# Strips of eight weight pieces: high and low passes ordered by pairs of pieces instead of by single pieces

## What is computed

```
block 1: proj   = x @ w_in                          # 2048 -> 12800
         r, i   = sigmoid(per-head u @ w_a), sigmoid(per-head u @ w_x)   # 20 heads, two directions
         h      = scans over time of (a(r), i*u)    # forward and backward
         merged = sig(g_lru) * (h @ w_lru_out) + sig(g_conv) * (conv @ w_conv_out)
         h1     = layer_norm(ALPHA*x + merged @ w_o)
         h2     = layer_norm(ALPHA*h1 + relu(h1 @ mlp_w1 + b1)**2 @ mlp_w2 + b2)
block 2: proj   = rms_norm(h2) @ w_in_2             # three attention / convolution branches
         x2     = h2 + mix @ w_out_2
         out    = x2 + (silu(n @ w_gate) * (n @ w_up)) @ w_down,   n = rms_norm(x2)
```

## Time and profile before

| what | us |
|---|---|
| median of three runs | 2660.29 (2658.74 to 2661.93) |
| the profiled execution, its own time | 2661.17 |
| its span in the trace | 2659.4 |
| busy: PE / DVE / ACT / POOL | 2641.6 / 1750.2 / 1349.3 / 34.5 |
| granted TensorE clock over the span | 0.999 of 2.4 GHz |

### The profile page before, as it was taken

How to read it: one execution, slowest core, us unless ns; L and a number is a source line. 1 busy time by engine, 2 the same in 40 slices (tenths; PEclk the granted TensorE clock), 3 DMA queues, 4 the chain that set the end, 5 groups by cost and what they waited for, 6 DMA issues and landing times.

```text
span 2659.4 us, 40669 instructions
## 1 busy us (share of the span) xinstructions
PE 2641.6 (99%) x14413; PEld 2290.7 (86%) x14413; DVE 1750.2 (66%) x1874; ACT 1349.3 (51%) x1540; POOL 34.5 (1%) x30
## 2 busy tenths in 40 slices
PE   9999999999999999999999999999999999999999
PEld 8888888888888888888888888889888888888888
DVE  7787877544454655555555567997666666666667
ACT  5667765444443544444444445566554444444444
POOL 0000000000000100000000001000000000000000
PEclk9999999999999999999999999999999999999999
DMA  7555555655655455556556654543555555555555
GB/s 261 184 181 185 191 188 194 199 180 189 203 178 176 155 191 191 180 189 204 190 176 193 202 192 154 174 135 129 175 188 189 189 189 189 189 189 189 189 189 168
DMA packets 133305, 491.91 MB, mean 185 GB/s; under 512 B 14800, under 2 KB 15312, under 8 KB 133200
## 3 DMA queue, kind: packets, MB, share of 16 engines
q1 hardware_dynamic: 133200, 490.52, 56.7%
HBM read 488.36 MB, written 2.10 MB: 184 GB/s over the span
## 4 chain that ended last, share of the span: by engine, by line
PE 93%; DVE 4%; issue 1%; ACT 1%; DMA 1%; SPq 0%; DVEq 0%; ACTq 0%
PE ps_a L373 18%; PE ps_b L373 18%; PE ps_a L382 9%; PE ps_b L382 9%; PE ps_b L465 6%; PE ps_b L467 6%; PE ps_b L466 6%; PE ps_a L465 5%; PE ps_a L466 5%; PE ps_a L467 5%; PE ps_b L777 1%; DVE w_lo L1305 1%; DMA w_raw<-w_dram 1%; DVE bconv L1799 1%; DVE gates L1451 1%
## 5 line engine op out<-in xcount | busy, mean ns | idle before, releaser
L1305 DVE TENSOR_TENSOR w_lo<-w_raw,w_hi 128x1024 fp32r<-128x1024 f32 (+1 forms) x908 | 1120.3, 1247 | 702.5 <-ACT w_hi L840 691.3
L840 ACT ACTIVATE w_hi<-w_raw 128x1024 fp32r<-128x1024 f32 (+1 forms) x908 | 970.7, 1075 | 1142.8 <-PE ps_b L467 244.6
L373 PE MATMUL ps_b<-xx,w_hi 128*128 128x512 f32 x1184 | 288.7, 391 | 4.8 <-DVE xx L1622 2.1
L373 PE MATMUL ps_a<-xx,w_hi 128*128 128x512 f32 x1120 | 271.6, 391 | 0.0
L373 PEld LDWEIGHTS ps_b<-xx,w_hi 128*128 128x128 f32 x1184 | 216.3, 188 | 48.0 <-issue 5.3
L373 PEld LDWEIGHTS ps_a<-xx,w_hi 128*128 128x128 f32 x1120 | 205.1, 188 | 39.2
L373 PE MATMUL ps_a<-x,w_hi 128*128 128x512 f32 x704 | 169.7, 391 | 0.0
L373 PE MATMUL ps_b<-x,w_hi 128*128 128x512 f32 x704 | 169.7, 391 | 0.0
L382 PEld LDWEIGHTS ps_b<-xx,w_lo 128*128 128x128 f32 x1184 | 153.4, 191 | 6.1
L382 PE MATMUL ps_b<-xx,w_lo 128*128 128x256 f32 x1184 | 157.1, 283 | 0.0
L373 PEld LDWEIGHTS ps_a<-x,w_hi 128*128 128x128 f32 x704 | 129.4, 188 | 25.0
(11 more groups left out here) (310 smaller groups left out, 3968.8 us busy)
## 6 DMA issues: line engine op xcount, KB each, us to landing
w_raw<-w_dram SPq DMA_DIRECT2D x836, 512.0 KB, 3.6
w_raw<-w_dram SPq DMA_DIRECT2D x72, 640.0 KB, 4.4
zz<-x_dram SPq DMA_DIRECT2D x8, 256.0 KB, 4.9
out_dram<-res SPq DMA_DIRECT2D x3, 512.0 KB, 2.8
out_dram<-res SPq DMA_DIRECT2D x4, 128.0 KB, 2.1
const<-const_dram SPq DMA_DIRECT2D x1, 449.0 KB, 5.2
prm<-prm_dram SPq DMA_DIRECT2D x1, 308.0 KB, 6.6
```

What stands on the lines that cost most here:

```text
L373: last = nc.tensor.matmul(group[:, j, :], w_hi[:, r, o * P:o * P + P], moving(src, at + k), start=k == 0, stop=end and k == kt - 1)
L840: act.activation(w_hi[:, r, 0:width], w_raw[:, r, 0:width], ACT.Copy).then_inc(hi_done, 1)
L1305: dve.tensor_tensor(w_lo[:, r, 0:width], w_raw[:, r, 0:width], w_hi[:, r, 0:width].bitcast(F32), ALU.subtract).then_inc(lo_even if r % 2 = ...
```

## The change

In the 53 strips the order of PE's passes goes by pairs of pieces: heavy p0, heavy p1, light p0, light p1, light p2, light p3, heavy p2, heavy p3, and the same again for p4 to p7. Runs inside a strip are 32 matmuls long, with 16 heavy ones at either end. `pe_piece` is raised four times for each half strip as before, now at the end of each piece's second pass. `start` goes to the pass that begins a piece and `stop` to the other. Strips with gates, strips of two pieces and the first strip keep their order. Nothing is changed on ACT, DVE, POOL and SP.

```diff
-                    if p % 2 == 0 or not turns:
-                        high(sorted(in_turn, key=lambda o: o[1][1]) if free_bank is not None and p == 0 else in_turn,
-                             need, False)
-                        last = low(nothing, True)
+                if gates_of is not None or not turns or len(pieces) == 2:
+                    for p in range(len(pieces)):
+                        if p % 2 == 0 or not turns:
+                            high(p, need, True)
+                            last = low(p, nothing, False)
+                        else:
+                            low(p, need, True)
+                            last = high(p, nothing, False)
+                        if gates_of is not None:
+                            last = gate_pair(gates_of, e, gates_in, p, slot(p)[1])
+                        last.then_inc(pe_piece, 1)
+                    return
+                for p in range(0, len(pieces), 2):
+                    if p % 4 == 0:
+                        high(p, need, True, free_bank is not None and p == 0)
+                        high(p + 1, need, True)
+                        low(p, nothing, False).then_inc(pe_piece, 1)
+                        low(p + 1, nothing, False).then_inc(pe_piece, 1)
                     else:
-                        low(need, False)
-                        last = high(in_turn, nothing, True)
-                    if gates_of is not None:
-                        last = gate_pair(gates_of, e, gates_in, p, r)
-                    last.then_inc(pe_piece, 1)
+                        low(p, need, True)
+                        low(p + 1, need, True)
+                        high(p, nothing, False).then_inc(pe_piece, 1)
+                        high(p + 1, nothing, False).then_inc(pe_piece, 1)
```

More of the change, by code:

```diff
@@ L360, in strip @@
                     free()
[L361 to L384, removed]
-                    if p % 2 == 0 or not turns:
-                        high(sorted(in_turn, key=lambda o: o[1][1]) if free_bank is not None and p == 0 else in_turn,
-                             need, False)
-                        last = low(nothing, True)
-                    else:
-                        low(need, False)
-                        last = high(in_turn, nothing, True)
-                    if gates_of is not None:
-                        last = gate_pair(gates_of, e, gates_in, p, r)
-                    last.then_inc(pe_piece, 1)
@@ new lines, in strip, with slot, high @@
+                pieces = [tiles[first:first + main] for first in range(0, len(tiles), main)]
+                def slot(p):
+                    return q + (p + r0) // 4, (p + r0) % 4
+                def high(p, needed, begins, by_bank=False):
+                    piece, r = slot(p)
+                    hi_ready(piece, r)
+                    order = list(enumerate(pieces[p]))
+                    for o, (k, j) in sorted(order, key=lambda o: o[1][1]) if by_bank else order:
+                        if j == 0:
+                            needed(k)
+                        if k == 0 and free_bank is not None:
+                            free_bank(j)
+                        last = nc.tensor.matmul(group[:, j, :], w_hi[:, r, o * P:o * P + P], moving(src, at + k),
+                                                start=begins and k == 0, stop=not begins and k == kt - 1)
+                    return last
@@ new lines, in low @@
+                def low(p, needed, begins):
+                    piece, r = slot(p)
+                    lo_ready(piece, r)
+                    for o, (k, j) in enumerate(pieces[p]):
+                        if j == 0:
+                            needed(k)
+                        last = nc.tensor.matmul(group[:, j, 0:S], w_lo[:, r, o * P:o * P + P],
+                                                moving(src, at + k)[:, 0:S], start=begins and k == 0,
+                                                stop=not begins and k == kt - 1)
+                    return last
```

## The result

The changed kernel takes 2668.6 us (median of 8 runs, 2667.4 to 2670.0), the kernel before 2661.5 us in the same series (8 runs, 2658.7 to 2664.3). The ratio is 1.0028, 95% interval 1.0019 to 1.0037: +7.2 us. The change makes the kernel slower; that it is slower by more than the prediction's 0.2% is likely but not certain, since the low end of the interval lies just under that. The profiled execution of the changed kernel took 2667.36 us around a span of 2665.6 us.

A forecast was written before the change was run, and what follows sets the result against it. PE bounds the kernel, busy 2641.6 of 2659.4 us. Terms -2.1 + 8.8 - 1.1 + 1.0 = +6.6 us on the profiled 2661.17 give 2667.8, or 2666.9 us against the median; range 2661 to 2670.5.

The forecast's parts named there:

- Part 1: All 53 strips: each loses two of its four turns from light to heavy matmuls, 0.02 us each, -2.1 us.
- Part 2: Recurrent stage: slot 0 handed back 1.8 us late moves the whole path to the gate product, +8.8 us over five rounds.
- The third strip's wait for p7: Recurrent stage, third strips: p7's light pass waits 0.6 us for its low part, not added in rounds ending on the sum.
- the 1.8: Recurrent stage, third strips: slot 0's delay of 1.8 us, expected to reach the gate product whole.
- the sum's slack of 1.0: Recurrent stage, round 2: the sum ends 1.0 us before PE's gate product at the loop's jump, making 2.2 into 1.2.
- Part 3: Output product, third strip: the 0.84 us stall before p4's light pass goes, -1.1 us, at worst 0.
- The start: Near the start: two waits go, but gate products behind wait for a sum fed by unmoved loads; 0, -0.6 at best.
- Part 4: First strip behind each norm: third low part wanted earlier, 0.4 and 0.6 us late, together +1.0 us, up to +2.7.
- (a): Recurrent stage absorbs the late slot; only turns, the stall and the norms count: -2.2, 2658.1 us; chance 0.12.
- (b): Recurrent stage: the delay reaches the sum only in part, +8.8 becomes +4.4: 2662.5 us; chance 0.20.
- (c): Feed-forward spare 0.6 us missing, 18 loop strips losing some 0.2 each, or norms at upper bound: 2670.5 us; chance 0.12.

The follow-up runs named there:

- doubled turns: The kernel before, with 42 strips outside the start and recurrent stage run heavy, light by single pieces, eight turns each: 2663.9 against 2661.9 us, ratio 1.0010.

## Why the prediction was right, point by point

**Part 1, turns: right.** -0.04 us a strip, 0.020 a turn behind runs of 8 as of 32. By the rule of columns / 2.4 + 2.5 ns, which the Trainium skill (TensorE: Matmul & The Clock Gate, "Back-to-back issue gap") gives for isolated matmuls, the doubled turns would have cost nothing. They cost 1.76 us in 90 turns. The -2.1 are not all to be seen: the recurrent strips' 0.4 drown in waits. In the other strips 1.5 us are measured: without turns the distance would end at 7.69 + 0.48 + 0.69 - 1.16 = 7.70, and it ends at 6.19.

**Part 2, the recurrent stage: right, in size and in mechanism.** +8.8 forecast, +8.7 in the trace and +8.8 when changed alone. By rounds: 2.2 each in 1, 3 and 4, as forecast; round 2 1.4 where I had 1.2; round 5 0.65 where I had 1.0, since its second strip does not wait. Two points were off inside a round. The third strip's wait for p7, 0.7 us, does lie inside the 1.8, as I had said, but as a part that comes earlier: the gate product then waits 1.1 more and not 1.8. And in round 2 the sum's slack of 1.0 is not what counts: the gap at the jump grew from 1.0 to 1.3 us and had the waits ahead of it added in full. That 1.4 is near 1.2 is partly luck.

**Part 3, the output product: right.** -1.1 forecast, 8.22 - 7.06 = -1.16. The light pass of the first slots behind the activations now starts after their low parts, with no idle time in its row:

```profile
1894.87 3.79 PE L376 MATMUL ps_a<-mixc,w_hi 128*128 128x512 f32 x16
1898.49 4.00 PE L387 MATMUL ps_a<-mixc,w_lo 128*128 128x256 f32 x32
```

All eight kernels that have the new order here show the same -1.16, whatever order the recurrent stage has; the four others with the old order here show 0.00 to -0.02.

**The start: the 0 stands, though the table says -0.97.** The two stalls of the earlier trace rows go wherever the second strip has the new order. But four kernels that leave the old order there lack them too (the new order in the ten strips alone, its first pair alone, the root first in the kernel before, doubled turns) and are 0.7 to 2.1 us ahead at 81.6 us; a fifth, with only the second strips changed, still has both. Over all kernels the distance at 81.6 us lies between -2.1 and +0.7 with the old order and between -1.0 and +0.3 with the new. It belongs to the execution, not to the order; the granted clock is full there in all of them, so what moves it stays open.

**Part 4, the norms: right, +0.48 and +0.69 in the table where +0.4 and +0.6 were forecast.** The wait behind the second norm is the one I had named, a light pass that waits for `w_lo` instead of a heavy one that waits for activations:

```profile
1627.95 1.22 PE L387 MATMUL ps_b<-xx,w_lo 128*128 128x256 f32 x8 [1.40 <-DVE w_lo L1324]
```

But this stretch differs by more than that between kernels whose order is the same there, and the granted clock goes with it. In all fourteen profiles PE idles about 3.25 us ahead of the transposes behind the second norm. In thirteen of them the clock is then at 1.2 GHz for some time. Where it is still down at the first heavy pass, eight matmuls take 3.75 us and not 2.09: first a pass and a window in the kernel with the first pair put back, then the same in the changed kernel (a window's row has PE's busy us and matmuls, the granted clock with 1.00 for 2.4 GHz, DMA share and GB/s).

```profile
1610.25 3.75 PE L376 MATMUL ps_b<-xx,w_hi 128*128 128x512 f32 x8 [0.96 <-DVE xx L1647]
1612.00:1613.00 1.00, 1.00 (x4) 0.50 0.00 0
...
1619.81 2.09 PE L376 MATMUL ps_b<-xx,w_hi 128*128 128x512 f32 x8 [1.22 <-DVE xx L1641]
1620.00:1621.00 1.00, 1.00 (x5) 1.00 0.00 0
```

Sorted by that time at 1.2 GHz, what the stretch behind the second norm takes beyond the profile of before falls into place:

| at 1.2 GHz | old order, us | new order, us |
|---|---|---|
| not at all | -0.7 (doubled turns) | no profile |
| about 3 us | 0 (before), 0.04 | 0.68 to 0.70 (four kernels, the changed one among them) |
| about 7 us | 0.99 to 1.02 (three kernels) | no profile |
| about 10 us | 2.20 and 2.21 | 2.86 and 2.91 |

At equal clock the new order costs 0.65 to 0.7 us. Behind the first norm, with the full clock throughout, it costs 0.47 (four kernels with the new order at 0.47 to 0.48; three with the old at 0, the doubled turns at 0.2). Where the clock fell there for about 3 us, the old order stands at 0.5 to 0.9 and the new at 1.2 and 1.4. That the two main profiles had the same clock at both norms is luck; from the pair alone the order and the clock could not have been told apart.

**Sum and rivals.** +6.6 forecast on the profiled execution, +6.2 measured between the two (2667.36 - 2661.17) and +7.2 between the medians. Rivals (a) and (b) let ACT or DVE absorb the delay: the distance of the sum moved by 1.8, whole. (c) asked for waits for `w_lo` in the feed-forward parts: there is none from 926 to 1600 us and none behind 1904 us.

What the prediction did not see is how little holds the loss together. It says that ACT takes its work in order, and stops there. The square root need not stand behind the waiting split, and with the root ahead of it the loss is gone, as the run with the root first shows. A gain over the kernel before with the same exchange is not shown (2659.0 against 2659.3 us).

## What to carry to other kernels

When an order on one engine hands a buffer back later, follow the first instruction that waits for it and list what stands behind it on its engine: here 1.8 us on one slot cost 6.5 us at three gate products and a loop's jump, and moving an unrelated square root ahead of the waiting split took it all away. Then change the single pair of instructions that the theory names, alone and in reverse; that settles more than undoing the stage. And do not read a step of under 1 us from one pair of profiles at a place where PE has idled (loads at the start, statistics of a norm): compare the granted clock of the stretch first, and look at the same step in kernels that do not differ there.

## What the runs showed of the hardware

**The clock can fall behind a short wait.** In the kernel with only the first pair new, the gate product of round 3 waits 1.91 us for the sum, like those of rounds 1 and 4 (1.90 and 1.96). Behind this one the granted clock drops to half, 1.2 GHz, for somewhat under 4 us, in the midst of work (window; PE's busy us and matmuls; PEclk; DMA share; GB/s):

```profile
278.00:279.00 1.00, 0.15 (x1) 1.00 0.95 358
279.00:280.00 1.00, 1.00 (x6) 0.51 0.85 287
280.00:281.00 1.00, 1.00 (x6) 0.50 0.80 225
281.00:282.00 1.00, 1.00 (x7) 0.50 0.70 287
282.00:283.00 1.00, 1.00 (x5) 0.78 0.18 72
```

It costs what this round loses beyond the others, 3.33 - 1.82 = 1.5 us. The waits of equal length in rounds 1 and 4 were followed by the full clock, and so were the changed kernel's of 1.2 and 1.3. The idle times at the norms are alike in all fourteen profiles, and there too the clock falls in some only: behind 2.25 us at the first norm in six, behind 3.25 us at the second in thirteen. Which of them it strikes stays open.

**The gap at the loop's jump hangs on what PE has in front of it.** From start to start, over the matmul's own 0.227 us, it is 0.9 to 1.3 us in the kernels whose third strip ends with one heavy pass, 2.2 in the one with the late slot besides; 0.3 or nothing where sixteen heavy matmuls stand there and the low parts are in time; but 1.4 and 1.5 in the changed kernel and in the one with only the ten strips changed, where sixteen stand there and the light pass ahead of them had to wait. That fits a jump that PE's queue can only make ready once its last wait is over; the one run that changed the end of the strip alone bears it out, but no run changed the wait alone, so this remains the likely reading and not a shown one.
